# Gate and up of three FFNs by seven half-size products per tile, with an adding DMA for gate's low half

## The reference, cut to what matters

```python
x = x + 0.5 * swiglu(rms_norm(x, n_ffn1[i]), gate1[i], up1[i], down1[i])
x = x + hybrid_mix(rms_norm(x, n_mix[i]), ...)
x = x + 0.5 * swiglu(rms_norm(x, n_ffn2[i]), gate2[i], up2[i], down2[i])
x = x + sigmoid(rms_norm(x, n_ple[i]) @ w_ple_gate[i]) * (p @ w_ple_proj[i])

def swiglu(x, wg, wu, wd):
    return (silu(x @ wg) * (x @ wu)) @ wd
```

## Time and profile before

| | us |
|---|---|
| median of three runs | 1988.18 |
| the profiled execution | 1987.9 |
| its span | 1986.2 |
| PE busy | 1961.6 (99%) |
| DVE busy | 1009.0 (51%) |
| ACT busy | 670.9 (34%) |
| POOL busy | 137.8 (7%) |

### The profile page before, as it was taken

How to read it: one execution, slowest core, us unless ns; L and a number is a source line. 1 busy time by engine, 2 the same in 40 slices (tenths; PEclk the granted TensorE clock), 3 DMA queues, 4 the chain that set the end, 5 groups by cost and what they waited for, 6 DMA issues and landing times.

```text
span 1986.2 us, 38193 instructions
## 1 busy us (share of the span) xinstructions
PE 1961.6 (99%) x16072; PEld 1942.6 (98%) x16072; DVE 1009.0 (51%) x1216; ACT 670.9 (34%) x848; POOL 137.8 (7%) x181
## 2 busy tenths in 40 slices
PE   7999999999999999999999999999999999999997
PEld 7999999998999999999999999999999999999996
DVE  6444434668554344346854244346775443443465
ACT  5222312445433122124433122124544331221353
POOL 1000000130110000001100000002201000000012
PEclk9999999999999999999999999999999999999998
DMA  5222222322332222223222222222222222222241
GB/s 205 86 97 93 84 96 94 108 84 66 106 119 95 96 85 95 85 95 129 95 85 95 90 91 95 85 95 98 76 94 96 95 91 90 87 94 89 92 139 44
DMA packets 54131, 190.46 MB, mean 96 GB/s; under 512 B 6096, under 2 KB 8432, under 8 KB 54048
## 3 DMA queue, kind: packets, MB, share of 16 engines
q1 hardware_dynamic: 52576, 184.87, 27.6%
q0 software_dynamic: 1472, 4.38, 0.7%
HBM read 186.91 MB, written 2.31 MB: 95 GB/s over the span
## 4 chain that ended last, share of the span: by engine, by line
PE 98%; DVE 1%; ACT 0%; DMA 0%; issue 0%; POOL 0%; DVEq 0%; SPq 0%; ACTq 0%
PE main L447 92%; PE aux L600 2%; PE aux L548 1%; PE aux L447 1%; PE main L504 1%; PE main L600 1%; PE aux L620 0%; PE aux L472 0%; PE main L673 0%; DVE x L1223 0%; DMA raw<-weights_dram 0%; DVE rstd_b L921 0%; DVE rstd_b L1218 0%; PE aux L623 0%; DVE part_lo L915 0%; PE aux L575 0%
## 5 line engine op out<-in xcount | busy, mean ns | idle before, releaser
L447 PE MATMUL main<-part_hi,w_hi 128*128 128x260 f32 x5056 | 1020.9, 283 | 1.9 <-DVE tmp L974 1.5
L447 PE MATMUL main<-part_hi,w_lo 128*128 128x260 f32 x5056 | 1019.4, 283 | 0.0
L447 PE MATMUL main<-part_lo,w_hi 128*128 128x260 f32 x5056 | 1017.2, 283 | 0.0
L447 PEld LDWEIGHTS main<-part_hi,w_hi 128*128 128x128 f32 x5056 | 780.3, 189 | 4.2 <-issue 2.7
L447 PEld LDWEIGHTS main<-part_hi,w_lo 128*128 128x128 f32 x5056 | 779.4, 189 | 0.0
L447 PEld LDWEIGHTS main<-part_lo,w_hi 128*128 128x128 f32 x5056 | 777.0, 188 | 0.0
L909 DVE TENSOR_TENSOR w_lo<-raw,w_hi 128x1024 fp32r<-128x1024 f32 (+1 forms) x344 | 433.2, 1260 | 206.8 <-ACT w_hi L696 195.0
L696 ACT ACTIVATE w_hi<-raw 128x1024 fp32r<-128x1024 f32 (+1 forms) x344 | 355.9, 1038 | 245.4 <-PE main L447 238.8
L739 ACT ACTIVATE part_hi<-tmp 128x520 f32 (+1 forms) x88 | 56.2, 639 | 433.9 <-DVE tmp L983 433.9
L734 ACT ACTIVATE tmp<-tmp 128x520 f32<-128x520 f32 x111 | 71.2, 642 | 357.4 <-DVE tmp L974 324.2
L1000 DVE SCALAR_TENSOR_TENSOR x<-main,x 128x520 f32<-128x520 f32 x96 | 66.8, 696 | 225.4 <-PE main L447 225.4
(11 more groups left out here) (180 smaller groups left out, 709.9 us busy)
## 6 DMA issues: line engine op xcount, KB each, us to landing
raw<-weights_dram SPq DMA_DIRECT2D x344, 512.0 KB, 3.2
x<-x_in_dram SPq DMA_DIRECT2D x4, 520.0 KB, 7.2
y_out<-x SPq DMA_DIRECT2D x8, 260.0 KB, 2.6
mix<-p_in_dram POOLq DMA_DIRECT2D x2, 520.0 KB, 3.6
ln<-ln_dram POOLq DMA_DIRECT2D x2, 512.0 KB, 3.9
ws<-ws_dram POOLq DMA_DIRECT2D x2, 512.0 KB, 5.7
bs<-bs_dram POOLq DMA_DIRECT2D x2, 256.0 KB, 3.9
bd<-bd_dram POOLq DMA_DIRECT2D x8, 64.0 KB, 6.2
```

The lines of the kernel that those rows point to most:

```text
L447: last = pe.matmul(ps[:, q, 0:HALF], ww[:, s, w], xx[:, k, q * HALF:(q + 1) * HALF], start=(a == 0 and b == 0), stop=(a == kts - 1 and b = ...
```

## The change

In three of the four FFNs (all but layer 0's first) gate and up of one hidden tile are computed together as the product of two 2 x 2 block matrices by a scheme of Strassen's kind (Winograd's form of it). On the one side are gate and up, each split in the lower and upper four of the 8 feature blocks; on the other x, split in the same feature halves and in the token halves A1 and A2. Seven products P1 to P7 of 4 blocks by 260 tokens take the place of eight. Each is 4 x 3 = 12 matmuls (`product`).

- The weight side of four products is a sum: tau1 = gate low half + up low half, tau2 = tau1 + up high half, tau3 = up low + up high, tau4 = tau2 + gate high ("low" and "high" of the feature blocks here). DVE adds them into `tau`, which shares its place with the mixer's `ln` and `ws`; ACT and DVE cut them (hi12 and lo12 for the first two, in weight slot 3; hi34 and lo34 for the others, in slot 2). The up high half is cut alone into `wx` (hi_b, lo_b).
- The gate unit itself (for P1 and P2) is cut without DVE: ACT copies raw to `w_hi` and minus raw, rounded, to `w_lo`; then POOL issues a DMA that adds the unit, read again from DRAM, into `w_lo` (`gate_low`, 512 KB per tile). P1 waits for it.
- The token side has four sums of x blocks (`sigma`), made and cut at the end of the stage before, in the last four feature tiles. P1 and P2 use x itself.
- Intermediate sums leave PSUM: ACT copies P1, U2 and P5 out, DVE adds them to later products (c11, c12, c22, c21). The sign of the up result is turned in `hidden`.
- The factor 1/rms on gate stays; that on up moves behind down: DVE now has two operations per down tile, a multiply by `rstd_b` and the update of x. The first down unit of a chunk starts between P7 and P4 of the last tile.
- POOL's load of layer 1's parameters moves behind that layer's first FFN, since `tau` holds their place, and the cut of the embedding input moves from behind the OUT stage to its third unit.
- The loops over tiles, which were hardware loops, are written out.

The core of the diff:

```diff
+def seven(l, which):
+    return (l, which) != (0, 0)
...
+        tau = sb("tau", [P, 2 * WA + 2 * MT * CHUNK])
+        ln = tau[:, 0:2 * WA].rearrange("p (a b) -> p a b", a=2)
+        ws = tau[:, 2 * WA:2 * WA + 2 * MT * CHUNK].rearrange("p (a b) -> p a b", a=2 * MT)
...
+            def gate_low(l, which, t):
+                T_ = first_tile(l, which) + t
+                c = 0 if t < FFN_CHUNKS[0] else 1 if t < sum(FFN_CHUNKS[:2]) else 2
+                n = l * UNITS + (U_F2 if which else U_F1) + 2 * t + c * XT
+                pool.wait_ge(gate_neg, T_ + 1)
+                pool.dma_start(w_lo[:, gate_slot(t), :], weights[n, :, :],
+                               accum_op=ALU.add).then_inc(gate_lo[gate_slot(t)], 16)
...
+            def product(ps, hi_w, lo_w, hi_x, lo_x, start, stop, k_wait=None):
+                for k in range(KH):
+                    if k_wait is not None:
+                        k_wait(k)
+                    w = slice(k * P, (k + 1) * P)
+                    for b, (ww, xx) in enumerate(((hi_w, hi_x), (hi_w, lo_x), (lo_w, hi_x))):
+                        last = pe.matmul(ps, ww[:, w], xx(k), start=(start and k == 0 and b == 0),
+                                         stop=(stop and k == KH - 1 and b == 2), skip_group_check=True)
+                return last
...
+                    def P1(t):
+                        if t < 2:
+                            pe.wait_ge(evac, G - 1 + t)
+                        else:
+                            pe.wait_ge(c21_ev, S + t - 1)
+                        pe.wait_ge(gate_lo[gate_slot(t)], 16 * ((S + t) // 2 + 1))
+                        kw = (lambda k: pe.wait_ge(xlo, XT * stat + k + 1)) if first and t == 0 else None
+                        product(X(G, t), *gate_w(t, 0), *a11, True, False, kw).then_inc(prod, 1)
+                    def P2(t):
+                        kw = (lambda k: pe.wait_ge(xlo, XT * stat + KH + k + 1)) if first and t == 0 else None
+                        product(Y(G, t), *gate_w(t, 1), *a12, True, True, kw).then_inc(prod, 1)
+                    def P6(t):
+                        pe.wait_ge(lo12_s, S + t + 1)
+                        pe.wait_ge(p1_copy, S + t + 1)
+                        if first and t == 0:
+                            pe.wait_ge(sx_lo, 2 * KH * (S // HT0 + 1))
+                        product(X(G, t), *slot_w(3, 1), *s2, False, False).then_inc(prod, 1)
+                    def P5(t):
+                        if t >= 2:
+                            pe.wait_ge(evac, G + 2 * t - 2)
+                        product(Z(G, t), *slot_w(3, 0), *s1, True, False).then_inc(prod, 1)
+                    def P7(t):
+                        pe.wait_ge(u2_copy, S + t + 1)
+                        pe.wait_ge(lo34_s, S + t + 1)
+                        product(X(G, t), *slot_w(2, 0), *s3, False, False).then_inc(prod, 1)
+                    def P4(t):
+                        pe.wait_ge(c22_ev, S + t + 1)
+                        product(X(G, t), *slot_w(2, 1), *a22, False, True).then_inc(prod, 1)
+                    def P3(t):
+                        pe.wait_ge(wlo, n + 2 * t + 2)
+                        product(Z(G, t), wx_hi, wx_lo, *s4, False, True).then_inc(unit, 2)
+                    P1(0)
+                    P1(1)
+                    P2(0)
+                    if first:
+                        stat1(stat)
+                    P2(1)
+                    P6(0)
+                    P5(0)
+                    P7(0)
+                    P4(0)
+                    P6(1)
+                    P5(1)
+                    P3(0)
+                    for g in range(1, tiles - 1):
+                        P1(g + 1)
+                        P7(g)
+                        P2(g + 1)
+                        P4(g)
+                        P6(g + 1)
+                        P5(g + 1)
+                        P3(g)
...
+                    P7(last_t)
+                    pe.wait_ge(dlo_s, 2 * (3 * (S // HT0) + c) + 1)
+                    if first:
+                        pe.wait_ge(std_s, stat + 1)
+                    down_part(0, 0, 2, True)
+                    P4(last_t)
+                    P3(last_t)
+                    down_part(0, 2, tiles, True).then_inc(unit, 1)
...
+            def seven_prep(stat, o):
...
+                cols = A1 if o < KH else slice(0, TOK)
+                act.activation(xparts(stat // 4)[0][:, o, cols], x[:, o, cols], ACT.Copy,
+                               scale=gain(stat, o)).then_inc(xhi, 1)
+                if o >= KH:
+                    k = o - KH
+                    act.wait_ge(sx_raw, 4 * (KH * f + k))
+                    act.activation(x21g, x[:, k, A2], ACT.Copy, scale=gain(stat, k)).then_inc(sx_t, 1)
...
+            def sigma_hi(stat, k):
+                f = first_tile(stat // 4, stat % 4 // 2) // HT0
+                act.wait_ge(sx_raw, 4 * (KH * f + k + 1))
+                act.activation(sig_all(k, False), sig_raw3, ACT.Copy).then_inc(sx_hi, 1)
+                act.activation(xparts(stat // 4)[0][:, k, A2], sig_raw(4), ACT.Copy).then_inc(sx_hi, 1)
+            def gate_cut(n, t, T_):
+                act.wait_ge(raw_in[n % SLOTS], 16 * (n // SLOTS + 1))
+                act.activation(w_hi[:, gate_slot(t), :], raw[:, n % SLOTS, :], ACT.Copy)
+                act.activation(w_lo[:, gate_slot(t), :], raw[:, n % SLOTS, :], ACT.Copy,
+                               scale=-1.0).then_inc(gate_neg, 1)
+            def hi12(n, T_):
+                act.wait_ge(t12, 2 * T_ + 2)
+                act.activation(w_hi[:, 3, :], tau12, ACT.Copy).then_inc(whi, 2)
+            def hi34(n, T_):
+                act.wait_ge(wlo, n + 1)
+                act.activation(w_hi[:, 2, :], tau34, ACT.Copy).then_inc(hi34_s, 1)
+            def hi_b(n, T_):
+                act.wait_ge(raw_in[(n + 1) % SLOTS], 16 * ((n + 1) // SLOTS + 1))
+                act.activation(wx_hi, raw_up(n, 1), ACT.Copy).then_inc(hib_s, 1)
...
+                        act.wait_ge(unit, n + 2 * g)
+                        hi_b(n + 2 * g, S + g)
+                        copy_p1(g + 1)
+                        h_hi(g - 1)
+                        done(g, "P4")
+                        hi34(n + 2 * g + 2, S + g + 1)
+                        silu(g)
+                        copy_u2(g + 1)
+                        gate(g + 3)
+                        copy_p5(g + 1)
+                        if g + 2 < tiles:
+                            hi12(n + 2 * g + 4, S + g + 2)
...
+            def sigma(stat, k):
...
+                    dve.wait_ge(sx_lo, 2 * at)
+                dve.scalar_tensor_tensor(sig_raw(1), x[:, k + KH, A2], gain(stat, k + KH), x21g,
+                                         ALU.mult, ALU.subtract).then_inc(sx_raw, 1)
+                dve.scalar_tensor_tensor(sig_raw(3), x[:, k, A1], gain(stat, k), x21g,
+                                         ALU.mult, ALU.subtract).then_inc(sx_raw, 1)
+                dve.wait_ge(sx_raw, 4 * at + 1)
+                dve.scalar_tensor_tensor(sig_raw(2), x[:, k, A1], neg_gain(stat, k), sig_raw(1),
+                                         ALU.mult, ALU.subtract).then_inc(sx_raw, 1)
+                dve.wait_ge(sx_raw, 4 * at + 3)
+                dve.scalar_tensor_tensor(sig_raw(4), x[:, k + KH, A1], neg_gain(stat, k + KH), sig_raw(2),
+                                         ALU.mult, ALU.subtract).then_inc(sx_raw, 1)
+            def sigma_lo(stat, k):
...
+                dve.wait_ge(sx_hi, 2 * at + 1)
+                dve.tensor_tensor(sig_all(k, True), sig_raw3, sig_all(k, False), ALU.subtract).then_inc(sx_lo, 1)
+                dve.wait_ge(sx_hi, 2 * at + 2)
+                dve.tensor_tensor(lo_[:, k, A2], sig_raw(4), hi_[:, k, A2], ALU.subtract).then_inc(sx_lo, 1)
+            def tau1(n, T_):
...
+                dve.tensor_tensor(tau[:, 0:HB], raw_gate(n, 0), raw_up(n, 0), ALU.add).then_inc(t12, 1)
+            def tau2(n, T_):
+                dve.wait_ge(t12, 2 * T_ + 1)
+                dve.wait_ge(wlo, n - 1)
+                dve.tensor_tensor(tau[:, HB:2 * HB], tau[:, 0:HB], raw_up(n, 1), ALU.add).then_inc(t12, 1)
+            def tau3(n, T_):
...
+                dve.tensor_tensor(tau[:, 2 * HB:3 * HB], raw_up(n, 0), raw_up(n, 1), ALU.add)
+            def tau4(n, T_):
+                dve.wait_ge(t12, 2 * T_ + 2)
+                dve.wait_ge(gate_neg, T_ + 1)
+                dve.tensor_tensor(tau[:, 3 * HB:4 * HB], tau[:, HB:2 * HB], raw_gate(n, 1), ALU.add).then_inc(wlo, 1)
+            def lo12(n, T_):
+                dve.wait_ge(whi, n + 2)
+                dve.tensor_tensor(w_lo[:, 3, :], tau12, w_hi[:, 3, :], ALU.subtract).then_inc(lo12_s, 1)
+            def lo34(n, T_):
+                dve.wait_ge(hi34_s, T_ + 1)
+                dve.tensor_tensor(w_lo[:, 2, :], tau34, w_hi[:, 2, :], ALU.subtract).then_inc(lo34_s, 1)
+            def lo_b(n, T_, units=1):
+                dve.wait_ge(hib_s, T_ + 1)
```

(113 more changed lines are left out.)

370 lines of the change are left out of this document (339 added, 31 removed).

## The result

The changed kernel takes **2004.0 us** (median of 4 runs, 2003.5 to 2009.2) where the kernel before takes 1988.3: ratio 1.0084, interval 1.0067 to 1.0102. It is 16 us slower; I had forecast 12 us faster. The profiled execution took 2009.2 (span 2007.4), against 1987.9. So of the 95.2 us of work that TensorE (PE) no longer has, 95.2 + 21.3 = 116.5 were lost again, all of it and more, in that execution, and 95.2 + 15.7 = 110.9 by the medians. The forecast was 83.6.

A forecast was written before the change was run, and what follows sets the result against it. TensorE, busy 99%, was taken to bound the kernel. Of 95.2 us saved, 26.4 + 9.8 + 28.7 + 15.7 + 3 = 83.6 are given back, 11.6 gained: 1976.6 us as a median, range 1925 to 2020.

The forecast's parts named there:

- TensorE's saving: Three changed FFNs: 792 fewer matmuls at 0.1202 us, 95.2 us less.
- The ring: FFN loops: tau4, gate load, ACT's cuts, lo12, c22, back to tau4 take 10.41 us per tile against PE's 10.10.
- so I add 0.25: 3.71 us: Loops: time from tau4's end to ACT's start, with 0.25 for the gate load standing behind the up load.
- the distance of 0.6: Loops: the up half's load is issued 0.6 us before the gate load.
- Adding transfers: Loops: POOL's adding DMAs lengthen the weight loads by 0.25 us in 39 intervals, 9.8 us.
- the 3.7 that the forecast allowed: Loops: adding transfers have the queues alone for 3.7 us; up to that the loads are not delayed.
- Rival (b): Loops: adding transfers hold queues over 3.7 us, gate load lands late, slower than before: 2006 or 2025 us; chance 0.17.
- Starts: Starts of the three FFNs: PE waits for DVE's extra sums, 7.2 us twice and 14.3 once, 28.7 us.
- Ends: Last down stages and what follows: one more DVE operation, pitch 5.2 us, costs 15.7 us.
- Clock: FFN starts: matmuls at 1.2 GHz after PE's waits cost 3 us for the three.
- Rival (c): Loops: DVE becomes the bound, slowed beside POOL by 0.5 us on each of 66 tiles: 2010 us; chance 0.05.
- A chance of 0.32 for slower: Whole kernel: probability given to a slower result, against 0.60 for faster and 0.08 for the same.

The follow-up runs named there:

- e2: Changed kernel with each adding transfer cut to 64 of 1024 columns, most of gate's low half left out: 1995.6 us, ratio 1.0038.
- e5: Changed kernel with all odd-numbered weight loads, the up halves among them, bringing only 64 of 1024 columns: 1969.8 us, ratio 0.9908.
- e3: Changed kernel with the adding transfers replaced by plain copies of the same 512 KB: 1997.5 us, ratio 1.0050.
- e11: e6 with gate tile 1 cut right behind gate tile 0 at a chunk's start and its adding transfer issued earlier: 1959.0 us, ratio 0.9846.
- e4: Changed kernel with unread 252-column matmuls ahead of PE's long waits at the FFN starts: 2009.6 us, ratio 1.0107.
- e6: Changed kernel with tau4 ahead of lo12 and, on its own counter, the gate load issued ahead of the up load: 1963.0 us, ratio 0.9871.
- e9: e6 with the unread fill matmuls of e4 ahead of the long waits at the FFN starts: 1958.1 us, ratio 0.9849.

## Why the prediction was wrong

- **TensorE's saving: right.** 792 matmuls at 0.120 us.
- **The ring: right in every member, wrong in one link, and that decided the sign.** The step that failed is "one load takes all 16 queues 1.55 us, so I add 0.25: 3.71 us", from tau4's end to ACT. Measured are 4.42 in e2 (606.37 to 610.79) and 4.82 in the changed kernel (619.01 to 623.83), with a median of 4.6 over its intervals; in e5, without the load ahead, the median is 3.66. That made 0.3 us per interval of what is 1.0 to 1.3. The 0.25 doesn't follow from the text's own figures: 1.55 less the distance of 0.6 is 0.95, with which the ring is 11.11 and the forecast 1976.6 + 39 x 0.70 = 2004. That this is the measured time is in part luck, as other terms were off both ways. The distance was wrong too: tau3 and tau4 stand between the two issues, 1.21 us. And the load behind is late by 1.1 (4.3 for 3.2), where 1.55 less 1.21 would be 0.34: the 27.6% of the earlier trace rows give the time that packets take, as a mean over the 16 engines, not how long a load keeps the next one waiting. The trace of before had the case itself, which I did not look for, because I took the median of 344 loads of which nearly all stand alone. Its SP loop issued two loads at 464.90 and 466.04:

```profile
464.90 1.47 SPq L326 DMA_DIRECT2D raw<-weights_dram  x2
```

```profile
DMA to landing us min/median/max: 3.3/3.9/4.5
```

  With 4.5 less 3.2 for the 0.25 the ring is 11.5; 39 intervals at 1.05 more are 41 us, and the forecast would have been about 2018, less the 9.8 for the adding transfers 2008: slower, on the right side.

  The Trainium skill ("DMA: Bandwidth & Descriptors", section "Queues, rings and completion order") says that each DMA engine takes descriptors in the order of their ring. The pair in e2 fits that: issued at 616.39 and 617.60, landed 3.2 and 4.3 us later.
- **Adding transfers: the size right (8.4 for 9.8), the place wrong.** They left the ring nearly alone and delayed P1(1) at the starts. Their queue time is (218.8 - 13.9) / 66 = 3.10 us each, from q0's 10.9% of 2007.4 and 0.7% of 1986.2 before, under the 3.7 that the forecast allowed. A plain one of the same size on the same queue takes (133.7 - 13.9) / 66 = 1.8 (e3, 6.7% of 1996.0), a weight load 1.55. The estimate from "Collectives: The Full Stack" of the Trainium skill was 3.1 and agrees; its half rate is a factor of 2, against 1.7 measured on the one queue. Rival (b) ended on the right side for a wrong reason: its sign, landings above 4.2, came true (4.46), but the adding transfers are not what holds the gate load up (4.40 in e2, and 2 us less of waits).
- **Starts: 28.7 forecast, 29.6 counted**, and PE's waits are 7.3 and 8.5 us behind the two mixers for 7.2 each, 12.3 behind the embedding gate for 14.3. But P1(1) waits 4.8 to 6.3 us of these for the second adding transfer, and P6(0) not at all for sigma_lo: the size is right with another releaser, which is in part luck. e11 shows that both orders end at about the same sum, since DVE is behind either way.
- **Ends: 15.7 forecast, 10.9 counted.** DVE's pitch in the last down stage is 5.16 for the 5.2 forecast; what follows behind it was overpriced.

```profile
916.37 0.69 DVE L1619 TENSOR_TENSOR tmp<-main,rstd_b 128x520 f32<-128x520 f32 x1
...
921.53 0.69 DVE L1619 TENSOR_TENSOR tmp<-main,rstd_b 128x520 f32<-128x520 f32 x1
```

- **Clock: 3 forecast, 17.8 counted, none of it won back by e4.** More matmuls ran at 1.2 GHz than I thought, but beside waits that were longer. Behind e6's edit the same fill is worth 4.8 (e9).
- **Rival (c)**, DVE as the bound, is refuted: it waits 97.3 us for hi12 alone, and e6 runs at PE's pace with the same work on DVE.
- **Small slips** that change no conclusion: 10.6 + 7.4 is 18.0, not 18.2, at the mixer's starts, and ACT's list adds up to 6.4 us at pitch, not 6.9.
- The range, 1925 to 2020, held the time, although the forecast had the wrong sign. A chance of 0.32 for slower was low, with 39 intervals hanging on one link whose like I had not looked up.

## What to carry to other kernels

Where a ring is within a few per cent of the bound, price each link from the row most like it, not from a median: look for the same transfer with the same neighbour. A buffer should be freed as early as its last reader allows, and its load issued ahead of loads that are less urgent; moving one half-size DVE operation and swapping two issues was worth 41 us, more than any other edit here. And a loss may lie beside a longer ring: the clock was worth nothing with the ring and 4.8 us without it, the adding transfers 8.4 and 8.1. Only a test in both versions tells which kind it is.
